# Hybrid decoder step on one core: projection in another order with rotation on GpSimd, expert numbers of the route on GpSimd, compress product with both tap halves in 128 columns

## What is computed

```python
def _rope(x, pos):                    # q and the three kinds of keys
    ...
    x1, x2 = xf[..., :half], xf[..., half:]
    return jnp.concatenate([x1 * cos - x2 * sin, x2 * cos + x1 * sin], axis=-1)

def _compress(k, pe, w1, w2):         # 32 taps in two halves of 16, over chunks of 16 rows
    ...
    for j in range(r):
        wj = w1[j * CMP_STRIDE:(j + 1) * CMP_STRIDE]
        part = jnp.einsum('bcsgd,sdh->bcgh', chunks, wj)[:, j:j + nb] + ...
        hid = part if hid is None else hid + part
    out = jax.nn.gelu(hid) @ w2

def _ssm(u, h0, lp):                  # 1024 complex states, a linear recurrence over 512 tokens
    a_bar = jnp.exp(lam * step)
    ...
    _, hs = lax.associative_scan(_scan_combine, (a_seq, bu), axis=1)

def one(hc):                          # experts: 8 heads, 16 numbers each
    v1, i1 = lax.top_k(s1, PEER_TOPK)
    v2, i2 = lax.top_k(s2, PEER_TOPK)
    sc, ci = lax.top_k(cand, PEER_TOPK)
    e = (jnp.take_along_axis(i1, ci // PEER_TOPK, axis=-1) * PEER_NKEYS
         + jnp.take_along_axis(i2, ci % PEER_TOPK, axis=-1))
```

## Time and profile before

| | us |
|---|---|
| median of 3 runs | 2303.77 (2302.38 to 2306.18) |
| the profiled execution | 2322.88 |
| its span | 2321.1 |
| busy in the span | PE 1731.1, DVE 1391.8, POOL 686.4, ACT 303.1 |
| memory read and written | 646.34 MB and 11.26 MB |

### The profile page before, as it was taken

How to read it: one execution, slowest core, us unless ns; L and a number is a source line. 1 busy time by engine, 2 the same in 40 slices (tenths; PEclk the granted TensorE clock), 3 DMA queues, 4 the chain that set the end, 5 groups by cost and what they waited for, 6 DMA issues and landing times.

```text
span 2321.1 us, 22486 instructions
## 1 busy us (share of the span) xinstructions
PE 1731.1 (75%) x7742; PEld 789.9 (34%) x7742; DVE 1391.8 (60%) x3444; ACT 303.1 (13%) x702; POOL 686.4 (30%) x828
## 2 busy tenths in 40 slices
PE   7998699987879955888877778556665566665666
PEld 6434576652257642445432434001000011010111
DVE  3899415541122294887555667895789645777544
ACT  3000222331110211222111111000000000000000
POOL 4930200015100303323333333334333333333331
PEclk9899889998999986989986889656555666666657
DMA  4002530025215319999999999999999999999996
GB/s 165 2 20 76 136 132 1 1 74 167 82 60 203 99 46 360 421 412 415 412 413 409 387 410 404 396 373 412 416 416 410 417 414 413 415 407 405 415 416 252
DMA packets 129885, 654.90 MB, mean 282 GB/s; under 512 B 22084, under 2 KB 37108, under 8 KB 59948
## 3 DMA queue, kind: packets, MB, share of 16 engines
q0 software_dynamic: 80000, 562.07, 60.1%
q1 hardware_dynamic: 49772, 91.39, 11.3%
HBM read 646.34 MB, written 11.26 MB: 283 GB/s over the span
## 4 chain that ended last, share of the span: by engine, by line
DMA 25%; PE 16%; DVE 11%; issue 7%; POOL 3%; ACT 0%; DVEq 0%; POOLq 0%; ACTq 0%
DMA ex_uv<-in_peer_uv,idxT 25%; PE ex_acc L2082 8%; DVE ex_uv L2203 4%; PE ex_hb L1985 3%; POOL ex_uv L1878 3%; PE ex_late L2055 1%; PE ex_late L2007 1%; DVE ch_ci L1572 1%; DVE ch_sc L1569 1%; PE ex_late L2035 1%; DVE ch_iu L1572 1%; PE ex_late L2022 1%; DVE ch_work L1576 1%; DVE ch_work L1606 1%; DVE ch_work L1609 1%
## 5 line engine op out<-in xcount | busy, mean ns | idle before, releaser
L2203 DVE SCALAR_TENSOR_TENSOR ex_uv<-ex_uv,ex_hb 128x1024 f32<-128x1024 f32 x520 | 628.2, 1219 | 428.9 <-DMA ex_uv<-in_peer_uv,idxT 334.8
L1878 POOL DMA_INDIRECT ex_uv<-in_peer_uv,idxT x520 | 493.5, 949 | 989.2 <-PE ex_acc L2082 798.1
L1985 PE MATMUL ex_hb<-ex_h_rows,spread 24*128 24x512 bf16 x1040 | 349.9, 495 | 428.1 <-DVE ex_uv L2203 398.6
L2082 PE MATMUL ex_acc<-ex_uv,wts 128*32 128x512 f32 x2080 | 419.7, 928 | 0.0
L1985 PEld LDWEIGHTS ex_hb<-ex_h_rows,spread 24*128 24x128 bf16 x1040 | 52.8, 99 | 756.7 <-DVE ex_uv L2203 596.7
L2324 ACT ACTIVATE ex_gelu<-ex_dots 128x4 f32<-128x4 f32 x130 | 26.7, 205 | 1126.6 <-DVE ex_uv L2203 1107.1
L2082 PEld LDWEIGHTS ex_acc<-ex_uv,wts 128*32 128x32 f32 x2080 | 74.5, 146 | 250.3 <-issue 250.3
L1064 POOL MEMSET de_qbd<- 128x576 f32 x1 | 0.6, 577 | 222.4 <-POOLq L99 222.4
L2055 PE MATMUL ex_late<-hx,ex_ring 128*128 128x264 f32 x256 | 66.0, 414 | 0.0
L1280 PE MATMUL dpo<-de_xT,de_kT 128*64 128x504 f32 x128 | 58.4, 1085 | 5.4 <-ACT de_xT L1120 4.6
L1715 PE MATMUL ro_pq<-hT,w_q 128*128 128x256 f32 x256 | 59.4, 387 | 1.6 <-POOL idxT L1665 1.6
(11 more groups left out here) (457 smaller groups left out, 2407.1 us busy)
## 6 DMA issues: line engine op xcount, KB each, us to landing
ex_ring<-in_late_w SPq DMA_DIRECT2D x24, 1024.0 KB
gate_ring<-in_w_in SPq DMA_DIRECT2D x6, 2048.0 KB, 7.9
ex_uv<-in_peer_uv,idxT POOLq DMA_INDIRECT x520
w_q<-in_peer_w_q SPq DMA_DIRECT2D x8, 1024.0 KB, 8.0
w_out<-in_w_out SPq DMA_DIRECT2D x2, 2048.0 KB, 16.7
ex_h_rows<-h_split SPq DMA_DIRECT2D x65, 48.0 KB
pr_x<-in_x_prompt SPq DMA_DIRECT2D x4, 512.0 KB, 5.3
gate_ring<-in_w_in_heads SPq DMA_DIRECT2D x1, 2048.0 KB
```

Of the source, the lines that this page charges most:

```text
L1878: pool.indirect_dma_start(uv[:, s % SLOTS].rearrange("p j n -> p (j n)"), None, table, bass.IndirectOffsetOnAxis(ap=S.idxT[:, t:t + 1], ax ...
L1985: last = pe.matmul(hb[s % 2][:, CHUNK * h:CHUNK * h + CHUNK], spread[p, k % LOAD, :], h_rows[p, l % 2, CHUNK * h:CHUNK * h + CHUNK], start ...
L2082: last = pe.matmul(acc[LANE * g:LANE * g + LANE, CHUNK * h:CHUNK * h + CHUNK], wts[:, s % (2 * BATCH), LANE - 1 - r:2 * LANE - 1 - r], uv[ ...
L2203: dve.scalar_tensor_tensor(out=rows_, in0=rows_, scalar=1.0, in1=hb[s % 2][:], op0=ALU.mult, op1=ALU.mult, accum_out=dots[:, B % 2, c:c + ...
```

## The change

**Project.** The rates' inputs are loaded first; ACT takes their exponentials between the transposed halves, DVE makes the rates after two tiles are normed. Half of the `u` groups (the first 256 tokens) come first, then the input matrices' transposes, two more groups, and the loop, in which `share` says how many groups follow each step. The samples' input products move to steps 11 to 14. The fifth tile's projection is done in four strips of 32 columns over two taps each, and a product with `sel` sums the strips. The last doubling of table 0 is on DVE. POOL rotates the queries and two kinds of keys when its tables are done; DVE keeps the window keys. The last states are computed once after eight steps rather than in each.
**Decode.** The product takes 8 pairs of taps by two heads, both tap halves of a pair side by side in 128 stationary columns, 512 columns moving; ACT and DVE copy the two banks, and four products with a piece of the unit matrix add the halves, one shifted by a chunk.
**Route.** `PORTIONS` has 2, 2, 2, 1 and 1 heads; for all but the last, POOL computes the expert numbers.

```diff
+        FIRST = 4
...
+        share = [2, 2, 2, 1, 1, 2, 2, 1, 1, 3, 3, 1, 1, 1, 1, 0]
+        begin = [FIRST + 2 + sum(share[:k]) for k in range(len(share) + 1)]
+        BUS_AT = 11
...
         @block.gpsimd
...
-                for k in range(STEPS):
+                for k in range(STEPS if u else STEPS - 1):
...
+            pool.wait_ge(E["padded"], 1)
+            pool.wait_ge(E["tables"], 32)
+            for c, c0, heads, tiles in ((1, 0, NH, (0, 3)), (1, 0, NH, (3, 5)), (2, C_K, NKV, (0, 5)),
+                                        (2, C_K + 2 * KVW, NKV, (0, 5))):
+                pool.wait_ge(E["z_kept"], ends[c])
...
+                pool.tensor_tensor(t_[0], x1, cb, ALU.mult)
+                pool.tensor_tensor(t_[1], x2, sb_, ALU.mult)
+                pool.tensor_tensor(t_[2], x2, cb, ALU.mult)
+                link(pool.tensor_tensor(t_[3], x1, sb_, ALU.mult))
+                link(pool.tensor_tensor(x1, t_[0], t_[1], ALU.subtract))
+                link(pool.tensor_tensor(x2, t_[2], t_[3], ALU.add))
...
+            normed(0)
+            normed(1)
             dve.wait_ge(E["exps"], 1)
...
+            for t in range(2, TILES):
+                normed(t)
...
+            dve.wait_ge(E["table_half"], 1)
...
+            tt(q1[:, 0], co[:, :, 0:n], pr, ALU.mult)
+            tt(q1[:, 1], si[:, :, 0:n], pi, ALU.mult)
+            tt(q1[:, 2], si[:, :, 0:n], pr, ALU.mult)
+            link(tt(q1[:, 3], co[:, :, 0:n], pi, ALU.mult))
+            tt(co[:, :, n:], q1[:, 0], q1[:, 1], ALU.subtract)
+            link(tt(si[:, :, n:], q1[:, 2], q1[:, 3], ALU.add))
...
-            for c0, heads in ((0, NH), (C_K, NKV), (C_K + 2 * KVW, NKV), (C_K + 4 * KVW, NKV)):
+            for c0, heads in ((C_K + 4 * KVW, NKV),):
...
         @block.tensor
...
+            for j in range(FIRST, begin[0]):
+                project(j)
+            for s in range(len(steps) + 2):
                 if s < len(steps):
                     inputs(s)
-                if 2 <= s < len(steps) + 2:
+                if s >= 2:
                     outputs(s - 2)
...
+                if s < len(share):
+                    for j in range(begin[s], begin[s + 1]):
+                        project(j)
+                if BUS_AT <= s < BUS_AT + 4:
+                    sample_inputs(s - BUS_AT)
...
-                for t in range(CMP_LEN // 2):
-                    for g in range(NKV):
-                        last = pe.matmul(po[HD * g:HD * g + HD, 0, 0:NB * NC_S], w1[:, a, t, :],
-                                         xT[:, :, g, t:t + CMP_STRIDE // 2 * (NC_S - 1) + 1:CMP_STRIDE // 2],
-                                         start=(t == 0), stop=(t == CMP_LEN // 2 - 1))
+                taps = CMP_STRIDE // 2
+                for t in range(taps):
+                    for g, bank in enumerate((ph[:], po[:, 1, :])):
+                        last = pe.matmul(bank, w1[:, a, t, :], xT[:, :, g, t:t + taps * NC_S + 1:taps],
+                                         start=(t == 0), stop=(t == taps - 1))
                 last.then_inc(E["hid_done"], 1)
+                pe.wait_ge(E["parts_kept"], 2 * a + 2)
+                for g in range(NKV):
+                    chunks = parts[:, g, :].rearrange("p (b c) -> p b c", b=NB)
+                    for w in range(2):
+                        last = pe.matmul(po[HD * g:HD * g + HD, 0, 0:NB * NC_S], S.ident[:, HD * w:HD * w + HD],
+                                         chunks[:, :, w:w + NC_S], start=(w == 0), stop=(w == 1))
+                last.then_inc(E["hid_summed"], 1)
...
-    PORTIONS = ((0, 4), (4, 2), (6, 2))
+    PORTIONS = ((0, 2), (2, 2), (4, 2), (6, 1), (7, 1))
...
+            for i, (first, count) in enumerate(PORTIONS[:-1]):
+                pool.wait_ge(E["halved"], i + 1)
...
+                for j in range(2):
+                    link(pool.tensor_tensor(terms, hf[:, j].unsqueeze(2).broadcast_to([P, n, TOPK]),
+                                            R.iota[:].unsqueeze(1).broadcast_to([P, n, TOPK]), ALU.subtract))
+                    link(pool.tensor_scalar(terms, terms, 0.0, None, ALU.is_equal))
+                    link(pool.tensor_tensor(hit, hit, f[:, :, j, :].unsqueeze(2).broadcast_to([P, count, TOPK, TOPK]),
+                                            ALU.mult))
+                    for w in (8, 4, 2):
+                        link(pool.tensor_tensor(terms[:, :, 0:w], terms[:, :, 0:w], terms[:, :, w:2 * w], ALU.add))
+                    link(pool.tensor_tensor(pick[:, j], terms[:, :, 0], terms[:, :, 1], ALU.add))
...
             pe.wait_ge(E["eg_ready"], 1)
+            pe.wait_ge(E["indexed"], len(PORTIONS) - 1)
             turn_choice(pe, S, E["eg_done"], pt[:, 0:2 * P])
```

More of the change, by code:

```diff
@@ L437, in _, with keep_turned @@
             act.activation(rstd[:], rstd[:], ACT.Sqrt).then_inc(E["root_ready"], 1)
-            for j in range(2 * TILES):
+            act.wait_ge(E["rates"], 16 * 4)
+            act.activation(ldt[:], ldt[:], ACT.Exp).then_inc(E["exps"], 1)
+            def keep_turned(j):
                 t, kh = divmod(j, 2)
@@ L445, in _ @@
                                ACT.Copy).then_inc(E["hT_ready"], 1)
[L446 to L447 removed]
+            for j in range(4):
+                keep_turned(j)
             act.wait_ge(E["a_scaled"], 1)
@@ L452, in _ @@
             act.activation(s4[:], th[:], ACT.Sin, scale=0.25).then_inc(E["sines"], 1)
+            for j in range(4, 2 * TILES):
+                keep_turned(j)
             def keep(j):
@@ L506, in project @@
                     pe.wait_ge(E["z_kept"], j - 2)
+                if h == "sum":
+                    pe.wait_ge(E["sel_ready"], 1)
+                    pe.wait_ge(E["z_kept"], groups.index((c, 4, "strips")) + 1)
+                    pe.matmul(ps[j % 3][0:NB, 0:n], sel[:], quarter[:, 0:n], start=True, stop=True).then_inc(E["z_done"], 1)
+                    return
+                if h == "strips":
+                    for kk in range(2):
+                        for g in range(4):
+                            k = 2 * g + kk
+                            last = pe.matmul(ps[j % 3][ROW * g:ROW * g + ROW, 0:n], S.hx[:, k, LATE_TOK - ROW:LATE_TOK],
+                                             ring[:, c % 2, k, 0:n], start=(kk == 0), stop=(kk == 1))
+                    last.then_inc(E["z_done"], 1)
+                    return
                 for k in range(KT):
```

171 lines of the change are left out of this document (119 added, 52 removed).

## The result

The changed kernel takes 2292.11 us (median, 2291.66 to 2293.31) against 2304.97 for the kernel before, ratio 0.9944 with a 95% interval of 0.993 to 0.9958: 12.9 us gained where 48.5 were forecast.

What follows compares the result with a forecast made beforehand. The experts stage, with DMA engines 0.99 busy, was taken as the bound and left alone, so earlier gains reach the end one for one: -16.1 - 19.3 - 13.1 = -48.5, from 2303.8 to 2255 us, range 2240 to 2273.

Steps and rivals of the forecast that it cites:

- Decode, forecast -19.3: Both compress products in decode: each 9.9 us shorter with 128 stationary columns, less 0.5 for the last values pages.
- So width is free and the two halves ran one behind the other: Decode, compress product: 128 stationary columns cost no more than 64, and the two heads ran in series; 9.9 us saved each.
- a loss of 4.7 us a product: Decode: if the two heads had run in parallel, the new compress product would lose 4.7 us, twice.
- Project, forecast -16.1: Project stage: earlier scan start and shorter tail, less the wait for tables and the rotation's contention; stage end at 247.9.
- the rotation's price: Project: POOL's rotation, 34 us beside the scan, slows DVE by 0.40 us per us, costing the scan 13.6 us.
- 25 us bound: Project: upper bound on the rotation's cost to the scan, if each POOL instruction shuts DVE out for its whole length.
- Route, forecast -13.1: Route: with the index on POOL, PE turns the numbers at 859.3 instead of 872.43; bounds -15.5 and -5.5.
- no collision (1): Project: POOL's rotation does not slow the scan, so 13.6 us come back: 2242; chance 0.14.
- a GpSimd rotation that outlasts the scan (4): Project: the barrier waits for POOL; no gain if its rotation takes 136 us; chance 0.05 with anything else on that side.
- The third: POOL slower than its table products say: rotation 50 us alone, scan loses 20, route gives 5.5: 2269; chance 0.11.
- Pages that hold decode (2): Decode: the second product waits for loads now back to back, so decode gives 9 to 10: 2265; chance 0.12.
- the small end of every term: Whole sum with project -5, decode -9.4 and route -5.5: -20, giving 2284.

Runs made afterwards that it cites:

- The swapped loops: Kernel before, compress product doing all 16 products of the first head, then all 16 of the second: 2371.01 us (single run) against 2323.96.

## Why the prediction was wrong

The sum against the median, the place of the whole gain ahead of an experts stage that keeps its length, and the order of waits were right. The profile's 19 us over the median did no harm: they are waits in the decode window of one kind of execution, and the gain is 12.3 us there and 12.9 elsewhere. Three terms of the sum were off, by 29.1, 5.5 and 4.4 us as measured alone:

**Decode, forecast -19.3, measured +9.8 alone and +7.9 beside the other parts: the step that failed.** It is the sentence "So width is free and the two halves ran one behind the other". It joined, whose products read every eighth element, to a row, whose products read elements side by side, and laid the equal 0.91 and 0.891 us to one cause. Two effects cancel there: the step doubles a product (1.84 against 0.86), and two halves of the array share the time (1.83 a pair, 1.70 a single). A wide product keeps the first and gives up the second. The rule that the prediction weighed, the Trainium skill, "TensorEngine Tiling (Array Packing)", section "Key Properties", that tiles of the array work in parallel, was set aside with "The record pace in rows 9 contradicts that". The swapped loops show that the trace agrees with the rule. By it the prediction worked out a loss of 4.7 us a product; the window shows 3.2 (257.20 - 250.80 = 6.4 for two), since the new product is 0.4 longer than the old and a copy and sums come behind it. With a loss of 9.4 in place of a gain of 19.3 the sum would have been -19.8, at 2284. That was a rival to be named, and the range ended at 2273.

**Project, forecast -16.1, measured -9.0 in the profile and -10.6 alone.** The first scan step (49.52 for 49.5) and step 6 (130.46 after a wait for POOL, for 129.8) came as worked out, and the tail took 9.9 us (245.05 to 254.96) for 9.6. The mis-sized term is the rotation's price, 13.6, measured 18.5. It was taken from step 0 as 0.40 us per us of POOL. What is kept is not that rate but the exchange of one instruction for one. Step 0 of the kernel before, the scans and the POOL instruction beside them:

```profile
70.60 5.55 DVE L374 TENSOR_TENSOR_SCAN pr_x<-pr_mag,pr_x 128x256 f32<-128x256 f32 x4
71.42 1.42 POOL L234 TENSOR_TENSOR sgT<-pr_tab,pr_pw 128x512 f32<-128x512 f32 x1
```

A scan took 1.39 us there, beside POOL instructions of 1.37 to 1.42; the rotation's were 2.1 long, so it took 2.15. The Trainium skill, "SBUF — State Buffer", section "Who interferes with whom", says that DVE with two inputs in SBUF contends with a GpSimd instruction that reads SBUF, and that DVE with at most one input in SBUF, outside its two-port modes, does not. The trace agrees (8.61 for four scans, 2.47 for four products from PSUM). The prediction kept full exclusion as its 25 us bound. Another 1.3 us are the linked instructions on the last column (243.78 to 245.05 in the trace), which were called paid for. With the 0.7 by which step 6 began late and 0.3 in the tail this makes 7.2, where 7.1 are missing.

**Route, forecast -13.1, measured -9.1 in the profile and -8.7 alone.** The mechanism was right, a size was not: POOL's compare takes 1.51 us for 512 elements and not 0.8, its product with the numbers 1.26 and not 1.04, and its short sums are dearer, so two heads take 13.7 us (819.63 to 833.31) for 11.7 and one head 9.6 (833.31 to 842.89) for 8.2; the third portion began 0.8 late. 2.0 + 1.4 + 0.8 = 4.2, where 4.0 are missing.

Of the rivals, no collision (1) and a GpSimd rotation that outlasts the scan (4) are refuted by the rows. The third had its direction right in route, and its cost of the scan nearly (20), by a longer rotation than there was. Pages that hold decode (2) were not put to the test by the changed kernel, whose product got no shorter; they, or what goes with them, do bind the kernels whose product did.

No luck hid the miss: the forecast of 2255 and its range were missed by 37 and 19 us. That the small end of every term also gives 2284 is chance, since none of those ends was a loss in decode.

## What to carry to other kernels

Before two rows are joined to one price, compare how each operand is laid out: a product over a stepped moving operand and one over a dense one have different prices, and a saving by shape can be eaten by the step. Read the granted clock beside a product's time, too. Count work moved to GpSimd beside DVE as one DVE instruction per GpSimd instruction, at the longer one's length, and put it where DVE waits or reads PSUM. When a rule of the Trainium skill and an inferred reading of a row disagree, as they did here over the two halves of the array, the sign of a term can hang on it; give the rule its chance and its time.
